# Latent attention: the fifth score product over 128 rows, the turned probabilities in the unit's own score banks, the maximum ahead of the copies on VectorE

## The reference

```
q_nope, q_pe = q[..., :128], q[..., 128:192]        # 4 heads, rotated positions in q_pe
k = concatenate([k_nope, broadcast(k_pe)], -1)      # 1280 keys: 1024 tokens and 256 of the context
s  = einsum('bqhd,bkhd->bhqk', qi, k) / sqrt(192)   # one block of 128 queries
pr = softmax(s, axis=-1)
o  = einsum('bhqk,bkhd->bqhd', pr, v)               # v has 128 columns per head
```

## Time and profile before

| | us |
|---|---|
| median of three runs | 3346.16 |
| the profiled execution | 3344.78 |
| its span in the profile | 3343.0 |
| TensorE busy (95% of the span) | 3163.2 |
| VectorE busy (44%) | 1454.5 |
| ScalarE busy (32%) | 1054.2 |
| GpSimd busy (11%) | 372.4 |

### The profile page before, as it was taken

One profiled execution on the slowest core, in us unless ns is written; L12 is line 12 of the kernel. 1 busy time (PEld: TensorE's weight loads), 2 busy tenths in 40 slices (PEclk: granted clock), 3 DMA queues, 4 the chain that ended last, 5 costly groups with the idle time before them and its releaser, 6 DMA issues.

```text
span 3343.0 us, 42666 instructions
## 1 busy us (share of the span) xinstructions
PE 3163.2 (95%) x18680; PEld 2433.8 (73%) x18680; DVE 1454.5 (44%) x2104; ACT 1054.2 (32%) x1616; POOL 372.4 (11%) x390
## 2 busy tenths in 40 slices
PE   6999999999899999999998988988889999999999
PEld 2456766666667888888887766777767888888887
DVE  6256634666444311113336444266753444344333
ACT  4243322444333211112213655334433322222211
POOL 1012202334212000000002100011111100000000
PEclk9999999999999999999999999999999999999999
DMA  6011110000023111111212200000012111110212
GB/s 245 32 63 64 63 67 22 17 13 16 10 76 142 48 51 51 51 51 51 76 45 89 85 16 36 19 6 2 3 63 106 60 42 47 51 51 32 101 46 74
DMA packets 35209, 182.33 MB, mean 55 GB/s; under 512 B 4261, under 2 KB 4261, under 8 KB 21584
## 3 DMA queue, kind: packets, MB, share of 16 engines
q1 hardware_dynamic: 22176, 133.18, 11.3%
q0 software_dynamic: 12848, 46.43, 3.6%
HBM read 161.63 MB, written 17.96 MB: 54 GB/s over the span
## 4 chain that ended last, share of the span: by engine, by line
PE 84%; DVE 9%; ACT 4%; DMA 1%; issue 1%; POOL 1%; DVEq 0%; POOLq 0%; ACTq 0%; SPq 0%
PE ps L548 17%; PE ps L550 17%; PE ps L549 17%; PE ps L538 10%; PE ps L687 4%; PE ps L751 3%; PE ps L592 2%; PE ps L1228 2%; DMA ar<-in_xT 1%; PE ps L651 1%; PE ps L1089 1%; PE ps L834 1%; PE ps L609 1%; DVE ar L2089 1%; DVE ar L2095 1%
## 5 line engine op out<-in xcount | busy, mean ns | idle before, releaser
L548 PE MATMUL ps<-r,r 128*128 128x512 f32 x2632 | 1035.1, 393 | 10.7 <-DVE r L2085 5.4
L549 PE MATMUL ps<-r,r 128*128 128x512 f32 x2632 | 1026.4, 390 | 0.0
L550 PE MATMUL ps<-r,r 128*128 128x512 f32 x2632 | 1026.3, 390 | 0.0
L548 PEld LDWEIGHTS ps<-r,r 128*128 128x128 f32 x2632 | 495.4, 188 | 125.4 <-issue 16.2
L549 PEld LDWEIGHTS ps<-r,r 128*128 128x128 f32 x2632 | 495.5, 188 | 104.6 <-issue 3.0
L550 PEld LDWEIGHTS ps<-r,r 128*128 128x128 f32 x2632 | 495.2, 188 | 103.6
L2078 DVE TENSOR_TENSOR r<-ar,r 128x1024 fp32r<-128x1024 f32 (+1 forms) x170 | 204.3, 1202 | 325.1 <-ACT r L1411 325.0
L1411 ACT ACTIVATE r<-ar 128x1024 fp32r<-128x1024 f32 (+1 forms) x170 | 174.4, 1033 | 535.3 <-PE ps L550 495.4
L1449 ACT ACTIVATE ar<-ps 128x256 f32<-128x256 f32 (+3 forms) x330 | 146.9, 470 | 534.6 <-PE ps L538 115.7
L538 PE MATMUL ps<-ar 128*128 128x128 f32 (+4 forms) x1460 | 245.7, 340 | 6.4 <-ACT ar L1449 3.3
L538 PEld LDWEIGHTS ps<-ar 128*128 128x128 f32 (+1 forms) x1460 | 190.8, 186 | 57.4 <-issue 31.8
(11 more groups left out here) (295 smaller groups left out, 3485.6 us busy)
## 6 DMA issues: line engine op xcount, KB each, us to landing
ar<-in_w_mod SPq DMA_DIRECT2D x24, 1024.0 KB, 4.9
ar<-in_w_gu SPq DMA_DIRECT2D x22, 1024.0 KB, 4.8
ar<-in_w_up SPq DMA_DIRECT2D x22, 1024.0 KB, 4.8
ar<-in_w_in SPq DMA_DIRECT2D x19, 1024.0 KB, 4.8
ar<-in_w_dn SPq DMA_DIRECT2D x32, 512.0 KB, 3.5
x<-ar POOLq DMA_DIRECT2D x48, 256.0 KB, 2.3
ar<-x POOLq DMA_DIRECT2D x24, 512.0 KB, 8.1
ar<-in_xT POOLq DMA_DIRECT2D x16, 512.0 KB, 13.8
```

What stands on the lines that cost most here:

```text
L548: M.matmul(o, whk, hi[k][:, a:a + n], start=k == 0, stop=False)
L549: M.matmul(o, whk, lo_[k][:, a:a + n], start=False, stop=False)
L550: ins = M.matmul(o, wlk, hi[k][:, a:a + n], start=False, stop=k == nk - 1)
```

## The change

Four edits. (1) The fifth score product takes all 128 rows of `low_pe` and of `kst`. Rows 64 to 127 of `low_pe` are zero; GpSimd sets them once in each of the two buffers, ahead of the first subtraction that uses the buffer. (2) The three blocks of turned probabilities of unit u go to banks 3 * (u % 2) + 0, 1 and 2, which held the scores of the same unit; the list of banks 6 and 7 is left to the values product. By `claim`, the scores of unit u+2 then wait for the copies out of these banks. (3) VectorE takes the maximum of unit u and its negated form ahead of the copies of unit u-1. (4) The definitions of the small columns move with it.

```diff
                     ins = dot(o[:, a:a + n], [(hi, keys), (hi, keys_lo), (low, keys), (both, kst[:, a:a + n]),
-                                              (low_pe[0:64, :], kst[0:64, a:a + n])])
+                                              (low_pe, kst[:, a:a + n])])
...
                     key = ("pt", u, a)
-                    o = claim(key, next_of(OT), (evac[(u + n_) % 2], key))
+                    o = claim(key, 3 * (u % 2) + n_, (evac[(u + n_) % 2], key))
...
             for u in range(34):
+                mx, nb, sm, rs = [st[:, 4 * (u % 8) + j:4 * (u % 8) + j + 1] for j in range(4)]
+                if u < 32:
+                    dve.wait_ge(*product.at(("s", u)))
+                    V.tensor_reduce(mx, bank(("s", u), TT), AX, ALU.max).then_inc(*v_step())
+                    dve.wait_ge(*v_step.last())
+                    V.tensor_scalar(nb, mx, -scale, None, ALU.mult).then_inc(*v_soft(("nb", u)))
                 if 1 <= u < 33:
                     w = u - 1
...
                             copy(("pt", w, a), Tb[w % 2][:, a:a + n], bank(("pt", w, a), n))
-                mx, nb, sm, rs = [st[:, 4 * (u % 8) + j:4 * (u % 8) + j + 1] for j in range(4)]
-                if u < 32:
-                    dve.wait_ge(*product.at(("s", u)))
-                    V.tensor_reduce(mx, bank(("s", u), TT), AX, ALU.max).then_inc(*v_step())
-                    dve.wait_ge(*v_step.last())
-                    V.tensor_scalar(nb, mx, -scale, None, ALU.mult).then_inc(*v_soft(("nb", u)))
...
             pool.wait_ge(*a_hi.at(("q", u)))
+            if u < 2:
+                G.memset(low_pe[64:128, :].bitcast(F32), 0.0).then_inc(*p_gate(("zeros", u)))
+                pool.wait_ge(*p_gate.at(("zeros", u)))
             G.tensor_tensor(low, qn[:, hh * 1024 + qb * 128:hh * 1024 + qb * 128 + 128], hi.bitcast(F32),
```

## The result

The changed kernel takes 3288.09 us (median of four runs, 3287.74 to 3291.65) against 3347.51 us for the kernel before in the same comparison (3344.83 to 3354.24): a ratio of 0.9822, 95% interval 0.9805 to 0.9839. The forecast was 3288 us, with a range of 3279 to 3305. The profiled execution took 3287.74 us around a span of 3285.9, which is 57.1 us less than before; the sum of the prediction said 57.5. That the two agree this well is partly luck: terms of the sum were off in opposite directions, and work outside the change ran 3.0 us longer in this execution. The rows show which. The medians lie 59.4 us apart.

A forecast was written before the change was run, and what follows sets the result against it. TensorE's own sequence was taken to bound the kernel. 28 attention units at 6.34 instead of 8.22 us (52.7), start 2.7 and end 2.05 take 57.5 us off 3344.8: 3287.3, given as 3288, range 3279 to 3305.

The forecast's parts named there:

- the sum of the prediction: Latent attention: 28 units from 8.22 to 6.34 us give 52.7, with start 2.7 and end 2.05: 57.5 us off.
- The 128-row product: Score products of each attention unit: without three drains by the 64-row product, 2.95 us instead of 4.10, 1.15 less.
- The banks: Transposes of each attention unit: no wait for a copy, ten take 1.17 us against 1.84; 0.7 to 0.8 us gone.
- VectorE's order: Copies behind the next unit's maximum in the attention: end 0.4 us before the scores need the banks, so hidden.
- The memset: GpSimd's first memset, ahead of the first subtraction at the attention's start: 0 to 1.3 us, taken as 0.45.
- The start: First attention units: transposes 2 start at 213.4 instead of 216.12, 2.7 us gained, 1 to 4 allowed.
- rival 3: Attention: new TensorE idle stretches at the start keep the clock at 1.2 GHz afterwards; whole stage there gives 3472 us; 3%.
- The end: From transposes 30 to the attention's last copy: 10.65 us instead of 12.7, 2.05 gained.

## Why the prediction was right, and where its terms were off

*The 128-row product.* Right: 4.10 to 2.89 us, 2.95 forecast. The rule of the Trainium skill ("TensorE: Matmul & The Clock Gate", What overlaps and what doesn't) that weight loads run beside matmuls only in another row group does not hold here: fifteen 128-row loads in 2.94 us beside their matmuls. "TensorEngine Tiling (Array Packing)", Key Properties, says that a change of tiling mode drains the engine; the gaps around the 64-row loads agree with it. What the engine does in them no run shows; what is shown is that they go with the 64 rows.

*The banks.* Right: the wait for a copy is gone. Ten transposes take 1.08 us, 1.17 forecast: I took the pitch from a block that began behind a 64-row product, whose first step took 0.165 us where the others take 0.109. With the scores' 0.06 this makes a unit 6.20 instead of 6.34, and 28 of them 56.6 us instead of 52.7. This was the largest error of the sum, 3.9 us, and it made the forecast too cautious.

*VectorE's order.* Right in mechanism and in its waits: the copies end 0.4 us ahead of the scores, the copy of the output waits 1.05 us, and VectorE idles 0.18 us before the next maximum. The forecast left open what the order itself brings; it is 0.14 us a unit with both other parts and 0.01 with the banks alone; with the padding alone it was not run. The price that the prediction put at 0, GpSimd's subtraction beside VectorE's scaling in every second unit, is 0.36 us, above its 0 to 0.3 (0.94 us instead of 0.58 in one row, the scaling unchanged at 0.89), and the slack covers it:

```profile
293.89 0.94 POOL L2945 TENSOR_TENSOR q<-ar,q 128x128 fp32r<-128x128 f32 x1 [4.22 <-ACT q L1516]
```

*The memset.* It takes 0.20 us and delays the first subtraction by 0.29, 0.45 forecast:

```profile
189.43 0.20 POOL L2943 MEMSET q<- 64x128 f32 x1 [125.04 <-ACT q L1516]
```

*The start.* This step failed in its working, though it stayed within its allowance of 1 to 4: 1.2 us gained instead of 2.7 (transposes 2 at 215.46 instead of 216.12, with the whole stage 0.56 us later). Two errors partly cancel. The first maximum started 2.2 us earlier against the stage's start (6.9 us after the first rounding instead of 9.1), not 0.9. The first scores met less of the low clock: its mean was 0.79 over 188 to 196 us, 0.60 before. And rival 3's mechanism, a low clock after new idle stretches, came true for one unit: scores 2 cost 2.5 us more than at 3.1 us. I had set it aside since no such fall followed waits of the same length in the middle of the attention; but those waits were at most 0.7 us between dense work, and here they are 1.35 and 2.32 us. Length alone does not explain it either. With the order alone TensorE waited 1.34 us in every second unit and once 2.02 us at the start, and the granted clock stayed at 1.00:

```profile
316.24 0.44 PE L651 MATMUL ps<-ar 128*128 128x128 f32 x2 [1.34 <-DVE ar L2089]
...
284.00:316.00 32.00, 27.74 (x157) 19.81 (x155) 16.70 (x29) 10.51 (x23) 4.15 (x7) 1.00 0.17 59
```

*The end.* Right: 10.5 us from transposes 30 to the last copy (389.06 to 399.58), 10.65 forecast and 12.7 before.

Sum: 56.6 + 1.2 + 2.2 = 60.0 us in the attention, where 57.5 was forecast. That the profiled span came out at the forecast is luck: the rest took 3.0 us more in this execution, 3074.9 us, and that is no price of the change, since in the second profile of the same kernel it took 3068.3, less than before the change. The last step of the sum was loose too: 3287.3 and the 1.4 us up to the median make 3288.7, for which 3288 was given.

## What to carry to other kernels

A matmul of fewer rows inside a stream of 128-row matmuls is not a saving: here each cost 0.4 us, and filling it with zeros took 35 us out of the attention by itself (41 us between the medians); look at the gaps between weight loads, since the busy share of TensorE was 95% before and after. When a copy out of PSUM releases TensorE, give the product a bank whose last reader is already done, and then put each engine's work in the order in which TensorE will ask for it; before that, the same order can cost (0.62 us a unit here). The unchanged rest of this program varied by 11.6 us between the profiled executions, so a difference of a few microseconds is read from the stage itself, not from the total.

## What the runs showed of the hardware

The rest of the program is the same work in all these kernels, and took 3067.5 to 3079.1 us in the profiled executions. The shortest had a mean granted clock of 0.986 and the longest 0.981. The last column of the table accounts for most of the difference: 88 us at the 1.2 GHz level go with 3067.5 us, 119 us with 3079.1, and a straight line through the fourteen profiles gives 0.41 us of time for each further microsecond at that level (correlation 0.98). One place of the gated scan had 3.3 us of it in one profile of the changed kernel and none in the other.

In scores 2 the clock was at the lower level for part of the time in all five profiles of the changed start with its idle stretches left in or only shortened, and in none of the three in which they were filled. Two profiles of one kernel had scores 2 at 5.67 and 4.71 us. What sets the moment of a fall stays open: the kernel with the padding alone idled 1.30, 1.25 and 0.92 us at its start, and its clock did not fall there.
